# Ones-matmuls in four stops of TensorE, and second-layer operands that start elsewhere

## What is computed

```python
def _hybrid_layer(x, c, ...):                       # first layer
    mod = jax.nn.silu(c) @ w_ada + b_ada            # (2048) @ (2048 x 6144)
    shift, scale, gate = jnp.split(mod, 3, axis=-1)
    h = _rms_norm(x, g_norm) * (1.0 + scale) + shift
    proj = h @ w_in
    ...                                             # two attentions, 8 heads each
    y = jnp.concatenate([ya, yb], axis=-1) @ w_out
    return x + gate * y

def second_block(x, meta_tokens, ...):              # second layer
    r = jnp.concatenate([meta, x], axis=1)          # 16 + 256 = 272 rows
    h = rmsnorm(r, mix_pre_g)
    mix = mixer_block(h, ...)                       # h @ w_in, attention, pooling, @ w_out
    r = r + rmsnorm(mix, mix_post_g)
    h = rmsnorm(r, ffn_pre_g)
    ff = conv_ffn(h, ...)                           # h @ w_up, conv over 3 rows, gelu, @ w_down
    r = r + rmsnorm(ff, ffn_post_g)
    return r[:, 16:]
```

## Time and profile before

| | us |
|---|---|
| median of 3 runs | 2112.21 |
| lowest, highest | 2111.88, 2116.84 |
| the profiled execution, its own time | 2107.04 |
| its span in the trace | 2105.2 |
| TensorE busy in the span | 1991.2 |
| VectorE, ScalarE busy | 1281.6, 989.8 |
| mean granted clock of TensorE | 0.975 |

### The profile page before, as it was taken

How to read it: one execution, slowest core, us unless ns; L and a number is a source line. 1 busy time by engine, 2 the same in 40 slices (tenths; PEclk the granted TensorE clock), 3 DMA queues, 4 the chain that set the end, 5 groups by cost and what they waited for, 6 DMA issues and landing times.

```text
span 2105.2 us, 38795 instructions
## 1 busy us (share of the span) xinstructions
PE 1991.2 (95%) x15084; PEld 1889.0 (90%) x15084; DVE 1281.6 (61%) x1565; ACT 989.8 (47%) x1429; POOL 144.6 (7%) x151
## 2 busy tenths in 40 slices
PE   4289999999999999999999998999999999999997
PEld 2189999999998999988989998899999999988885
DVE  7886886675666544444457654655665665654544
ACT  3055555555644544444445454644444444444443
POOL 0000000000002000000004221000000000000000
PEclk8599999999999999999999999999999999999998
DMA  9966665575555566545444555366566656655553
GB/s 376 349 210 235 245 200 159 168 273 157 158 183 154 174 177 178 162 140 146 143 139 153 191 186 170 92 184 183 171 185 185 180 176 185 205 188 185 186 189 120
DMA packets 179903, 391.62 MB, mean 186 GB/s; under 512 B 11955, under 2 KB 17632, under 8 KB 177376
## 3 DMA queue, kind: packets, MB, share of 16 engines
q1 hardware_dynamic: 178800, 388.03, 58.0%
q10 hardware_dynamic: 1024, 2.51, 0.3%
HBM read 388.39 MB, written 2.10 MB: 185 GB/s over the span
## 4 chain that ended last, share of the span: by engine, by line
PE 90%; DVE 6%; ACT 2%; issue 1%; DMA 1%; SPq 0%; DVEq 0%; POOLq 0%; POOL 0%; ACTq 0%
PE acc L761 20%; PE acc L762 20%; PE acc L763 20%; PE psum_y L762 2%; PE psum_x L761 2%; PE psum_x L763 2%; PE psum_y L763 2%; PE psum_y L761 2%; PE psum_x L762 2%; DVE ada_acc L1665 2%; PE acc L1131 2%; PE acc L1130 2%; PE acc L1129 2%; DMA ada_w<-in_w_ada 1%; DVE ada_first L1665 1%
## 5 line engine op out<-in xcount | busy, mean ns | idle before, releaser
L1671 DVE TENSOR_TENSOR w_lo<-raw,w_hi 128x1024 fp32r<-128x1024 f32 (+1 forms) x644 | 813.5, 1271 | 712.6 <-ACT w_hi L1178 709.0
L1178 ACT ACTIVATE w_hi<-raw 128x1024 fp32r<-128x1024 f32 (+1 forms) x644 | 675.2, 1050 | 899.0 <-PE acc L763 580.5
L761 PE MATMUL acc<-act_hi,w_lo 128*128 128x258 f32 (+2 forms) x3424 | 978.5, 286 | 17.2 <-issue 9.3
L762 PE MATMUL acc<-act_lo,w_hi 128*128 128x258 f32 (+2 forms) x3424 | 968.3, 283 | 0.0
L763 PE MATMUL acc<-act_hi,w_hi 128*128 128x258 f32 (+2 forms) x3424 | 968.0, 283 | 0.0
L761 PEld LDWEIGHTS acc<-act_hi,w_lo 128*128 128x128 f32 x3424 | 651.8, 190 | 28.1 <-issue 26.6
L762 PEld LDWEIGHTS acc<-act_lo,w_hi 128*128 128x128 f32 x3424 | 651.1, 190 | 0.7 <-issue 0.5
L763 PEld LDWEIGHTS acc<-act_hi,w_hi 128*128 128x128 f32 x3424 | 650.6, 190 | 0.0
L762 PE MATMUL psum_y<-act_lo,w_hi 128*128 128x258 f32 x352 | 100.7, 286 | 0.0
L761 PE MATMUL psum_x<-act_hi,w_lo 128*128 128x258 f32 x352 | 100.4, 285 | 0.0
L763 PE MATMUL psum_x<-act_hi,w_hi 128*128 128x258 f32 x352 | 100.3, 285 | 0.0
(11 more groups left out here) (293 smaller groups left out, 2186.1 us busy)
## 6 DMA issues: line engine op xcount, KB each, us to landing
raw<-in_w_in SPq DMA_DIRECT2D x272, 512.0 KB, 3.7
raw<-in_w_ffn_up SPq DMA_DIRECT2D x176, 512.0 KB, 3.8
raw<-in_w_ffn_down SPq DMA_DIRECT2D x88, 512.0 KB, 3.6
raw<-in_w_out SPq DMA_DIRECT2D x64, 512.0 KB, 4.2
raw<-in_w_ada SPq DMA_DIRECT2D x32, 512.0 KB, 8.4
ada_w<-in_w_ada SPq DMA_DIRECT2D x32, 512.0 KB, 8.3
ada_x<-in_w_ada SPq DMA_DIRECT2D x16, 1024.0 KB, 6.4
raw<-in_w_attn_o SPq DMA_DIRECT2D x16, 512.0 KB, 3.6
```

The costliest lines, as they stand in the source:

```text
L761: pe.matmul(out, w_lo, a_hi, start=c == 0, stop=False)
L762: pe.matmul(out, w_hi, a_lo, start=False, stop=False)
L1178: act.activation(M.hi[s][:, 0:job.width], M.raw[s][:, 0:job.width], ACT.Copy).then_inc(M.hi_ready[s], 1)
L1671: dve.tensor_tensor(M.lo[s][:, 0:job.width], M.raw[s][:, 0:job.width], M.hi[s][:, 0:job.width].bitcast(FP32), ALU.subtract).then_inc(M.lo_ ...
```

## The change

It has three parts.

1. A helper `keep_busy(count)` issues plain fp32 matmuls of the tile of ones with itself, 128 by 256, into the first 256 columns of `psum_y`, which nobody reads. It stands at five places: 5 of them before the last group of column sums, behind two waits (60 of 64 chunks added up; the second set of columns copied out of PSUM), 6 after that group, 9 before qkv2, 15 between the second `live_sums` and the row sums of L1080, 9 after these.
2. pool_w, pool_o, out2 and up take their 258 columns from element 14 (`LIVE0`) of each block of `act2`, and ACT and DVE write them there: the start moves by 56 bytes, to 120 modulo 256.
3. `STILL` is 64 instead of 192: `d_hi`, `d_lo` and the three tiles behind them lie 128 bytes lower.

```diff
-STILL = 192
+STILL = 64
...
-        Job("pool_w", 1, 4, lambda i, j: pool_w[j], lambda k: act2(k, 0, LIVE), LIVE, 2, 256),
+        Job("pool_w", 1, 4, lambda i, j: pool_w[j], lambda k: act2(k, LIVE0, LIVE), LIVE, 2, 256),
...
-        Job("pool_o", 4, 4, cols(w_po, 0), lambda k: act2(8 + k, 0, LIVE), LIVE),
-        Job("out2", 4, 8, cols(w_out2, 0), lambda k: act2(k, 0, LIVE), LIVE),
-        Job("up", 22, 8, None, lambda k: act2(k, 0, LIVE), LIVE),
+        Job("pool_o", 4, 4, cols(w_po, 0), lambda k: act2(8 + k, LIVE0, LIVE), LIVE),
+        Job("out2", 4, 8, cols(w_out2, 0), lambda k: act2(k, LIVE0, LIVE), LIVE),
+        Job("up", 22, 8, None, lambda k: act2(k, LIVE0, LIVE), LIVE),
...
+    def keep_busy(count):
+        for n in range(count):
+            pe.matmul(M.Y[:, 0:SEQ], ones[:, 0:P], ones[:, 0:SEQ], start=True, stop=True)
+
...
     for g in range(4):
+        if g == 3:
+            pe.wait_ge(M.cols, 2)
+            pe.wait_ge(M.adaw_used, 4 * DC - 4)
+            keep_busy(5)
         pe.wait_ge(M.adaw_used, DC * (g + 1))
...
+    keep_busy(6)
     panel(job["qidx0"], 0, acts=M.mk["qidx0"])
...
     live_sums(13, 12)
+    keep_busy(9)
     q = job["qkv2"]
...
     live_sums(26, 28, LIVE0)
+    keep_busy(15)
     for k in range(DC):
...
         ins.then_inc(M.xsum, 1)
+    keep_busy(9)
...
     def hi2_of(k, n):
-        return M.act2_hi[:, PITCH * k:PITCH * k + n]
+        return M.act2_hi[:, PITCH * k + ROWS - n:PITCH * k + ROWS]
...
-    part2_hi = lambda k, n: M.act2_hi[:, PITCH * k:PITCH * k + n].bitcast(FP32)
-    part2_lo = lambda k, n: M.act2_lo[:, PITCH * k:PITCH * k + n]
+    part2_hi = lambda k, n: M.act2_hi[:, PITCH * k + ROWS - n:PITCH * k + ROWS].bitcast(FP32)
+    part2_lo = lambda k, n: M.act2_lo[:, PITCH * k + ROWS - n:PITCH * k + ROWS]
```

## The result

The changed kernel takes 2099.2 us (median of 5 runs, 2094.8 to 2102.1), the one before 2112.2 us (5 runs, 2110.7 to 2116.8). The ratio is 0.9933, with a 95% interval of 0.9918 to 0.9947: 0.7% faster, 11 to 17 us. The two medians lie 13.0 us apart; the ratio, which is not the quotient of the medians, makes it 14.1 us. The forecast was 2098.8 us, and that it came so near is luck: two of its terms were wrong by some 4 us each, in opposite directions.

A forecast was written before the change was run, and what follows sets the result against it. TensorE was taken to bound the kernel, busy 1991.2 of 2105.2 us. Fillers 4.2, moved right-hand sides 9.2 and d_hi/d_lo 0 made 13.4 us off 2112.2 us: 2098.8 us, range 2089 to 2109 us.

The forecast's parts named there:

- Second and fourth stop: TensorE's waits before qkv2 and before up: 9 fillers each keep the clock high, gaining 2.0 and 1.4 us.
- rival F: Fillers do not hold the clock: 4.2 us back, 2103.0 us; chance 0.07.
- First stop: Around w_ada's last column sums: five fillers gain 1.6 us or 0, 0.8 taken; six after are free.
- Third stop: Before L1080's row sums: 15 fillers speed the first 8 records by 1.9 us, but gain 0 overall.
- The moved right-hand sides: pool_w, pool_o, out2 and up reach g2's 119.0 ns pace: 9.2 us, of which up 7.4 us.
- d_hi and d_lo: down's stationary operands at a new start: 0 taken as the middle between 7.0 us less and 6.9 us more.
- rival B: down gains too, its weights' new start giving the best pace: 7.0 us less, 2091.8 us; chance 0.16.
- D: Rival: down loses 6.9 us, total 2105.7 us; chance 0.10.
- E: Rival: down's weight loads no longer hide fully, costing 19.9 us, total 2118.7 us; chance 0.05.
- The rule: Two independent SBUF read ports: operand starts change nothing, so the moved right-hand sides' 9.2 us would be 0.
- The sum: Whole kernel: fillers 4.2, moved right-hand sides 9.2, d_hi and d_lo 0, together 13.4 us less.

The follow-up runs named there:

- e6: Changed kernel with only the two groups of 9 fillers; the 5, 6 and 15 left out: 2098.1 us, ratio 0.9936.
- e4: Changed kernel without any fillers, both moves of operands kept: 2100.6 us, ratio 0.9953 to the kernel before.
- e1: Kernel before plus the fillers alone, operands starting where they did: 2106.4 us, ratio 0.9979.
- e7: Changed kernel with 10 fillers for 5, started earlier, 4 more among the L1080 row sums, 3 in the gate columns: 2096.0 us, ratio 0.9922.
- e10: Changed kernel plus ones-matmuls before up's second panel, out_a and down, and e7's fillers at the first and third stop: 2093.0 us, ratio 0.9919.
- e2: Kernel before with only the right-hand sides of pool_w, pool_o, out2 and up moved to element 14: 2106.9 us, ratio 0.9981.
- e5: Changed kernel with one more ones-matmul right before up's second panel: 2092.3 us, ratio 0.9909.
- e12: The e5 kernel with the right-hand sides of pool_w, pool_o, out2 and up back at element 0: one run, 2109.1 us.
- e3: Kernel before with only STILL at 64, moving d_hi, d_lo and the three tiles behind them: 2107.8 us, ratio 0.9983.

## Why the prediction was right, and where it was not

**Second and fourth stop.** Right: 2.0 and 1.4 us forecast, 2.1 and 1.3 us by the traces; the clock stayed at 1.00 through both, so rival F is out, and e6 against e4, with intervals that overlap, gives 3.6 us for the two.

**First stop.** The half (0.8 us) was a fair reading: the clock came up in time in four of seven traces, and in e1's, the nearest kernel, that saved 1.6 us. The end of the first panel was rightly left to ACT and DVE.

**Third stop.** The step "gain 0" looked only at the first 8 records. It took the 5.49 us of the 24 behind them as a constant, and these are on the path: 7.17 us in this trace, 1.7 us lost, because the clock was 0.50 for 3.4 us of them. The earlier 8 lengthened the wait ahead of the 24 from 0.60 to 2.40 us, but that wait alone does not decide it: e1 has it and 5.49 us, e6 has 0.60 us and 7.56 us. Without these fillers the 24 also took 7.3 to 7.9 us in three of five traces. What makes the clock fall there stays open; only the four further fillers of e7 and e10 went with 5.49 us both times.

**The moved right-hand sides.** The mechanism was right and the size off: 9.2 us forecast, 5.4 us by the traces, 4.0 us by e2. pool_o and out2 did what the forecast said, 1.65 ns a matmul. The term that failed is up's 7.4 us: 1.8 ns were carried from g2's stretches of 46 matmuls to one of 4055, and that one kept a second pace of the same addresses, 120.0 ns, 0.83 ns below before. The forecast named this carry-over as what could go wrong most. e5 shows that 119.05 ns is there to be had; with e12 both halves of the term are measured, address 0.83 ns and restart 0.95 ns.

**d_hi and d_lo.** Forecast 0 with bounds of 7 us either way; it was 4.4 ns a matmul, 4.7 us by the trace and 3.6 us by e3, on rival B's side; D and E, a slower down, are out. "The middle" was no reading but the lack of one: no row had this start. In e12's trace the same start gave nothing, 233.3 ns, so the gain need not come in every kernel, nor perhaps in every execution.

**The rule.** By the Trainium skill (TensorE: Matmul & The Clock Gate, the steps of a matmul) loading weights takes nothing from the running matmul. No run shows what waits for what inside the engine, but that the start of either operand leaves the pace alone, as I concluded from the rule, is refuted: by e2 for the moving operand (ten traces against four, without exception), and for the stationary one by e3 and by eight traces of nine against none of five.

**The sum.** 13.4 us forecast and 13.0 us measured agree by luck: 3.8 us too much in one term and 4.7 us too little in another cancel. The fillers alone were forecast at 4.2 us and measured at 4.4 us.

## What to carry to other kernels

Fill a stop of TensorE only where the work behind it is bound by TensorE and the filler ends just ahead of it; a filler that only brings other work forward moves the stop to a later place, where the clock can be down all the same. In a kernel that is one long stream of matmuls, read the step from start to start of each stage to a tenth of a nanosecond: a start address or one odd matmul ahead of a long stage can be worth as much as all the stops. And a diff is to be priced line by line: here one changed constant, `STILL`, went with a quarter of the gain. One trace of a kernel shows one execution; a pace is to be called settled only when it repeats, as up's does and down's does not quite.

## What was not expected of the hardware

- One shape at one clock has several exact paces, and keeps one for thousands of matmuls: 258 columns 119.05, 120.00 or 120.83 ns, 256 columns 113.3 or 117.8 ns, 272 columns 123.3 or 126.7 ns, 512 columns 228.9 or 233.3 ns. Which one is taken goes without exception with start address and restart in up (14 traces), and with the start address in 13 of 14 traces in down; for qkv2 it stays open. Why the paces exist is open too.
- The 16 one-column products of the gate (32 records, 3.6 to 4.9 us) did not hold the clock, although TensorE was busy throughout: in 11 of 14 traces it fell to 0.50 in their second half or up to 1.1 us behind them, for 3.4 to 6.8 us.
- Ones-matmuls of 256 columns kept the clock at 1.00 through the second and the fourth stop in all ten traces that have them there. They do not do so everywhere: behind the last column sums it fell in five of the six traces in which it had just come up, within 1 us of the start of the six fillers and for 3.4 to 6.8 us. That cost at most 0.5 us, since ACT and DVE set the end of this panel.
